# Weight chunks split in pieces, and three stage starts taken row by row, in a two-block attention, convolution and mLSTM kernel

## What is computed

```python
# first block
h   = rms_norm(x, g_pre) * (1 + scale) + shift        # scale, shift, gate = c @ w_ada + b_ada
proj = h @ w_in                                        # queries, keys, values, gates, z, merge
o_a, o_b = attention over compressed, selected and windowed keys, and a second windowed one
y   = (sigmoid(m_a) * ((o_a * silu(z_a)) @ w_o_nsa)
       + sigmoid(m_b) * ((o_b * silu(z_b)) @ w_o_swa)) @ w_out
x   = x + gate * rms_norm(y, g_post)
# second block, on [16 meta tokens; x], 528 tokens
u   = rms_norm(x, norm_w[0])
b, c, xin, z = split(u @ conv_in_w, 4)                 # 1024 -> 4 * 2048
x   = x + (silu(z) * b * causal_conv3(c * xin)) @ conv_out_w
u   = rms_norm(x, norm_w[1]);  x = x + mlstm(u)        # 4 heads, projections 1024 -> 8192
out = rms_norm(x, final_norm_w)[16:]
```

## Time and profile before

| | us |
|---|---|
| median of 3 runs (range) | 1727.71 (1726.42 to 1729.01) |
| the profiled execution, its own time | 1728.46 |
| its span, first to last instruction | 1726.7 |
| PE busy | 1636.3 |
| DVE / POOL / ACT busy | 750.3 / 606.0 / 536.5 |
| mean granted TensorE clock | 0.968 |

### The profile page before, as it was taken

One profiled execution on the slowest core, in us unless ns is written; L12 is line 12 of the kernel. 1 busy time (PEld: TensorE's weight loads), 2 busy tenths in 40 slices (PEclk: granted clock), 3 DMA queues, 4 the chain that ended last, 5 costly groups with the idle time before them and its releaser, 6 DMA issues.

```text
span 1726.7 us, 25059 instructions
## 1 busy us (share of the span) xinstructions
PE 1636.3 (95%) x9782; PEld 1415.2 (82%) x9782; DVE 750.3 (43%) x1489; ACT 536.5 (31%) x842; POOL 606.0 (35%) x485
## 2 busy tenths in 40 slices
PE   5898999999989989999999999989999999999996
PEld 5676777777767789999999999978788778878885
DVE  5705455554565753333233321232632462262255
ACT  2332333233332343222332222232332342233232
POOL 3454212222215423344434344233243244324332
PEclk9999999999989969999999999989999999999998
DMA  8132111111113401222222222222122122112111
GB/s 330 73 115 81 50 49 49 49 49 49 49 73 116 176 25 74 96 97 90 80 83 87 97 82 89 73 74 74 49 80 76 63 73 93 53 51 95 73 49 73
DMA packets 22738, 140.56 MB, mean 81 GB/s; under 512 B 3248, under 2 KB 3248, under 8 KB 6448
## 3 DMA queue, kind: packets, MB, share of 16 engines
q1 hardware_dynamic: 18752, 131.08, 20.6%
q10 hardware_dynamic: 3952, 9.00, 1.4%
HBM read 137.98 MB, written 2.10 MB: 81 GB/s over the span
## 4 chain that ended last, share of the span: by engine, by line
issue 40%; PE 37%; POOL 17%; DVE 4%; ACT 1%; POOLq 0%; DVEq 0%; ACTq 0%
PE lin L365 31%; POOL w_lo L311 17%; PE aux L788 3%; PE aux L760 1%; DVE mix L1466 1%; PE aux L746 1%; ACT w_hi L353 0%; PE aux L442 0%; DVE squares L1484 0%; PE aux L399 0%; PE aux L716 0%; PE aux L748 0%; DVE tmp L1405 0%; DVE residual L1509 0%; ACT mix L1019 0%
## 5 line engine op out<-in xcount | busy, mean ns | idle before, releaser
L311 POOL TENSOR_TENSOR w_lo<-w_raw,w_hi 128x512 fp32r<-128x512 f32 x460 | 602.3, 1341 | 1102.2 <-ACT w_hi L353 1102.2
L365 PE MATMUL lin<-x_hi,w_hi 128*128 128x272 f32 (+1 forms) x2128 | 590.6, 331 | 24.3 <-POOL w_lo L311 17.0
L365 PE MATMUL lin<-x_lo,w_hi 128*128 128x272 f32 (+1 forms) x2128 | 579.4, 326 | 0.0
L365 PE MATMUL lin<-x_hi,w_lo 128*128 128x272 f32 (+1 forms) x2128 | 578.1, 326 | 0.0
L365 PEld LDWEIGHTS lin<-x_hi,w_hi 128*128 128x128 f32 x2128 | 358.7, 192 | 71.1 <-issue 18.2
L365 PEld LDWEIGHTS lin<-x_hi,w_lo 128*128 128x128 f32 x2128 | 358.1, 192 | 32.5
L365 PEld LDWEIGHTS lin<-x_lo,w_hi 128*128 128x128 f32 x2128 | 358.6, 192 | 28.0
L353 ACT ACTIVATE w_hi<-w_raw 128x2048 fp32r<-128x2048 f32 x115 | 219.4, 1909 | 162.1 <-PE lin L365 156.6
L860 ACT ACTIVATE prob<-prob,neg_max 128x31 f32<-128x31 f32 (+6 forms) x128 | 60.1, 471 | 157.5 <-DVE neg_max L1196 157.5
L1317 DVE TENSOR_TENSOR conv_in<-conv_c_gate,lin 128x272 f32<-128x272 f32 (+1 forms) x32 | 12.3, 427 | 213.8 <-PE lin L365 213.8
L365 PE MATMUL lin<-mix,w_hi 128*128 128x512 f32 x256 | 81.9, 401 | 10.6 <-DVE mix L1466 7.1
(11 more groups left out here) (293 smaller groups left out, 1924.4 us busy)
## 6 DMA issues: line engine op xcount, KB each, us to landing
w_raw<-wstream SPq DMA_DIRECT2D x115, 1024.0 KB, 4.8
ada_shift_scale<-w_ada SPq DMA_DIRECT2D x8, 1024.0 KB, 19.1
ada_gate<-w_ada_gate ACTq DMA_DIRECT2D x4, 1024.0 KB, 5.7
residual<-x_t SPq DMA_DIRECT2D x1, 2048.0 KB, 8.9
residual<-x_t ACTq DMA_DIRECT2D x1, 2048.0 KB, 8.4
out_t<-residual ACTq DMA_DIRECT2D x8, 256.0 KB, 2.1
small_inputs<-smalls ACTq DMA_DIRECT2D x1, 537.0 KB, 3.5
residual<-meta_t ACTq DMA_DIRECT2D x1, 64.0 KB, 11.1
```

The lines of the kernel that those rows point to most:

```text
L311: ins = eng.tensor_tensor(wlo[h][:, cols], raw[h][:, cols], whi[h][:, cols].bitcast(F32), ALU.subtract)
L365: ins = t.matmul(o, w[half][:, c0:c0 + P], x(k, t0, cnt), start=(n == 0), stop=(n == 3 * kts - 1))
```

## The change

It makes the weights usable in pieces. ACT's high part becomes 2 instructions of 1024 columns, each with its own count in `s_hi`. POOL's four low parts stay as they are, but each adds 1 to `s_lo`, and POOL waits for the second half of `w_hi` only ahead of its third. PE waits for a piece ahead of each second row k in the first tile of a chunk (each fourth row, or each row, where a chunk has 16 or 4 rows), in place of one wait ahead of the chunk. SP's waits are counted in fours and mean the same.

It takes three stage starts row by row over more tiles. In the first projection both tiles are fed from one row before the next. In wo, the first chunk's tiles m = 0 and m = 1 are, with the second in other PSUM banks. In cin, both tiles of chunk 0 and, three rows behind, the first tile of chunk 1 are, and all this starts when the first row is ready, ahead of the norm. The squares of that norm are then kept (in the space of y), added up on DVE after the last row (eight instructions), turned into a column by PE in the middle of chunk 1's second tile, and spread after it. ACT splits chunk 1 of cin ahead of its work on the rows. DVE's copy of the norm factors of y (L449, there) is gone: it reads them from PSUM and puts the scaled y into PSUM. The first trip of cin is written out, the loop has 7.

The core of the diff, with the same edit elsewhere left out:

```diff
+HIGH_PIECES, PIECES = 2, 4
...
-                    eng.wait_ge(s_lo, i * 2 + (h + 1))
+                    eng.wait_ge(s_lo, i * (2 * PIECES) + PIECES * (h + 1))
...
+            def low_parts(h, first, i=0, per=0):
+                for p in range(PIECES):
+                    if p % (PIECES // HIGH_PIECES) == 0:
+                        eng.wait_ge(s_hi, i * (HIGH_PIECES * per) + (HIGH_PIECES * first + p * HIGH_PIECES // PIECES + 1))
+                    cols = slice(CHUNK // PIECES * p, CHUNK // PIECES * (p + 1))
+                    eng.tensor_tensor(wlo[h][:, cols], raw[h][:, cols], whi[h][:, cols].bitcast(F32),
+                                      ALU.subtract).then_inc(s_lo, 1)
...
-            a.activation(whi[h][:], raw[h][:], ACT.Copy).then_inc(s_hi, 1)
+            for p in range(HIGH_PIECES):
+                cols = slice(CHUNK // HIGH_PIECES * p, CHUNK // HIGH_PIECES * (p + 1))
+                a.activation(whi[h][:, cols], raw[h][:, cols], ACT.Copy).then_inc(s_hi, 1)
...
+            def rows_ready(first, rows, i=0, per=0, then=None):
+                def before(k):
+                    if k % rows == 0:
+                        eng.wait_ge(s_lo, i * (PIECES * per) + (PIECES * first + k // rows + 1))
+                    if then:
+                        then(k)
+                return before
...
+                ready = rows_ready(START["proj"] + c, 2)
+                if first:
+                    for k in range(KD):
+                        ready(k)
+                        eng.wait_ge(s_xlo, k + 1)
+                        for g in range(2):
+                            ins = group(eng, c % 2, g * P, 256, KD, lin_outs(g, TB1), x_hi, x_lo, ks=[k])
...
+            for x in range(2):
+                for k in range(4):
+                    eng.wait_ge(s_og_lo, 4 * x + k + 1)
+                    for m in range(2):
+                        ins = wo_tile(0, m, x, ks=[k])
...
-            growing_totals_pe(eng, n2, TB2, T2)
-            norm_spread_pe(eng, n2, TB2)
+            LAG = 3
+            for k in range(KD + LAG):
+                if k < KD:
+                    eng.wait_ge(s_ulo, k + 1)
+                    for g in range(2):
+                        ins = cin_tile(0, g, ks=[k])
...
+                if k >= LAG:
+                    ins = cin_tile(1, 0, ks=[k - LAG])
+            ins.then_inc(s_cin_tile, 1)
+            cin_tile(1, 1, before=second_norm).then_inc(s_chunk, 1)
+            eng.wait_ge(s_conv_in, 1 + CREDIT)
+            norm_spread_pe(eng, n2, TB2, bank=0)
...
+            chunk_lands_and_splits(eng, START["cin"] + 1)
             for k in range(KD):
                 eng.wait_ge(s_x1, k + 1)
                 act(xhi[:, k, :], res[:, k, :], ACT.Copy, scale=norm_c[:, 0, k:k + 1]).then_inc(s_uhi, 1)
-                if k >= 2:
-                    eng.wait_ge(n2.added, k - 1)
-                act(sq[:, k % 2, :], res[:, k, :], ACT.Square).then_inc(n2.squared, 1)
-            grown_root_act(eng, n2, TB2, D)
+                act(m_a[:, k, :], res[:, k, META:T2], ACT.Square).then_inc(n2.squared, 1)
+            act(meta_sq, res[:, :, 0:META], ACT.Square).then_inc(n2.squared, 1)
...
+            gates_out(0, 0)
+            chunk_lands_and_splits(eng, START["cin"] + 2)
+            norm_root_act(eng, n2, TB2, D, bank=n2_total)
+            conv_out(0, 0)
+            chunk_lands_and_splits(eng, START["cin"] + 3)
+            gates_out(0, 2)
...
-            norm_rstd_dve(eng, own, n1, TB1)
+            eng.wait_ge(n1.spread, 1)
...
-                own.up(stt(tmp[:, k % 2, 0:T1], m_a[:, k, :], gpost[:, k:k + 1], rstd[:, 0:T1], ALU.mult, ALU.mult))
+                own.up(stt(aux[3][:], m_a[:, k, :], gpost[:, k:k + 1], aux[2][:], ALU.mult, ALU.mult))
```

More of the change, by code:

```diff
@@ L497, in project @@
                         eng.wait_ge(s_q, g + 1)
-                    elif not first:
+                    else:
                         eng.wait_ge(s_proj_out, 2 * (at - 1) + g + 1)
-                    ins = group(eng, c % 2, g * P, 256, KD, lin_outs(g, TB1), x_hi, x_lo,
-                                before=(lambda k: eng.wait_ge(s_xlo, k + 1)) if first and g == 0 else None)
+                    ins = group(eng, c % 2, g * P, 256, KD, lin_outs(g, TB1), x_hi, x_lo, before=None if g else ready)
                     ins.then_inc(s_chunk if g else s_proj, 1)
@@ L682, in _, with cin_tile, second_norm, cin_trip @@
             norm_spread_pe(eng, n1, TB1)
-            growing_totals_pe(eng, n2, TB2, T2)
-            norm_spread_pe(eng, n2, TB2)
-            with eng.bass.Fori(0, 8, 1, engines=[eng.engine]) as ii:
-                for c in range(4):
-                    chunk_ready(START["cin"] + c, ii, 4)
+            def cin_tile(c, g, ks=None, before=None):
+                return group(eng, c % 2, g * P, 256, KD, cin_outs(c, g), x_hi, x_lo, ks,
+                             before if g else rows_ready(START["cin"] + c, 2))
+            def second_norm(k):
+                if k == 4:
+                    eng.wait_ge(s_cbc_out, 1)
+                    norm_total_pe(eng, n2, TB2, KD, bank=n2_total)
+            LAG = 3
[4 more added lines that the diff above has]
+                        ins = cin_tile(0, g, ks=[k])
+                        if k == KD - 1:
+                            ins.then_inc(s_chunk if g else s_cin_tile, 1)
+                if k >= LAG:
[4 more added lines that the diff above has]
+            norm_spread_pe(eng, n2, TB2, bank=0)
+            def cin_trip(ii, cs):
+                for c in cs:
+                    ready = rows_ready(START["cin"] + c, 2, ii, 4)
                     for g in range(2):
@@ L695, in _, with last_rows @@
                             eng.wait_ge(s_conv_in, ii * 4 + ({0: -1, 1: 0, 4: 1, 5: 2}[j] + CREDIT))
[L696 to L697 removed]
+                        ins = group(eng, c % 2, g * P, 256, KD, lin_outs(g, TB2), x_hi, x_lo, before=None if g else ready)
                         ins.then_inc(s_chunk if g else s_cin_tile, 1)
+            for g in range(2):
+                eng.wait_ge(s_cbc_out, g + 1)
+                cin_tile(2, g).then_inc(s_chunk if g else s_cin_tile, 1)
+            cin_trip(0, range(3, 4))
+            with eng.bass.Fori(1, 8, 1, engines=[eng.engine]) as ii:
+                cin_trip(ii, range(4))
+            def last_rows(k):
+                if k >= KE - 2:
+                    eng.wait_ge(s_vlo, k + 1)
             with eng.bass.Fori(0, 2, 1, engines=[eng.engine]) as ii:
                 for c in range(4):
[L701 removed]
                     if c < 2:
@@ new lines, in gates_out @@
+            def gates_out(ii, c):
+                u = c // 2
+                for g, dst in ((0, cb), (1, cc)):
+                    if g == 1:
+                        eng.wait_ge(s_chunk, ii * 4 + (START["cin"] + c + 1))
+                    else:
+                        eng.wait_ge(s_cin_tile, ii * 4 + (c + 1))
+                    eng.wait_ge(s_conv, ii * 2 + (u + CREDIT))
+                    for b, t0, n in TB2:
+                        ins = act(dst[:, t0:t0 + n], lin[g][:, b, 0:n], ACT.Copy)
+                    ins.then_inc(s_cbc_out, 1)
@@ L1301, in _ @@
             low_u(KD - 1)
+            eng.wait_ge(n2.squared, 2)
+            own.up(tt(ssum[:, META:T2], m_a[:, 0, :], m_a[:, 1, :], ALU.add))
+            for k in range(2, KD):
+                eng.wait_ge(n2.squared, k + 1)
+                own.settle()
+                own.up(tt(ssum[:, META:T2], ssum[:, META:T2], m_a[:, k, :], ALU.add))
+            own.settle()
+            eng.wait_ge(n2.squared, KD + 1)
+            eng.tensor_reduce(ssum[:, 0:META], meta_sq.rearrange("p k n -> p n k"), AX.X, ALU.add).then_inc(n2.added, KD - 1)
@@ L1340, in _ @@
+                    conv_in(ii, u, [lin[0][:, b, :] for b in range(2)])
+                    conv_rest(ii, u, [lin[1][:, b, :] for b in range(2)])
                 own.leave(8)
```

218 lines of the change are left out of this document (110 added, 108 removed).

## The result

| | before | after |
|---|---|---|
| median of the runs, us | 1727.55 (1726.42 to 1729.01, 4 runs) | 1684.35 (1682.91 to 1686.08, 4 runs) |
| ratio after to before, 95% interval | | 0.975 (0.9739 to 0.9762) |
| profiled execution, us (span) | 1728.46 (1726.7) | 1686.08 (1684.3) |
| mean granted clock | 0.968 | 0.979 |

A forecast was written before the change was run, and what follows sets the result against it. PE's matmul time was taken as the floor, leaving its idle time and half clock to win. Terms 8.0 + 1.6 + 6.3 + 3.9 + 2.2 + 0.8 + 13.1 = 35.9 us gave 1692 us, range 1682 to 1706.

The forecast's parts named there:

- part 4: Start of cin: rows taken up ahead of the norm, PE starting at 610.5 and bound by itself; gain 13.1 us.
- part 3: First chunk of wo: two tiles fed row by row gain 1.85 us, 1.1 lost to DVE; net 0.8 us.
- part 2: First projection: both tiles fed row by row, PE ending at 59.0 instead of 61.2; gain 2.2 us.
- Part 1: Weights in pieces: PE's waits for POOL of 4.18 us at 80.15 and 3.85 at 100.89 both go, 8.0 us.
- 1.6 us at 145.08: First attention group: of a 3.11 us wait for POOL only 1.6 us go, the first exponential being PE's next need.
- 6.3 us for cin's seven waits: Trips 2 to 8 of cin: seven waits for POOL, 0.9 us each by the starts, all go; 6.3 us.
- 3.9 us for the clock behind the long waits: Behind the two long waits in the first block, half-clock losses of 2.2 and 1.7 us go with the idle time.
- Costs at nothing: Some 345 added waits on PE, and ACT's second start of 0.1 us for each of 115 chunks, were costed at nothing.
- A: Rival: the clock stays low through cin's row-by-row start, price 12 us, 1704 us; chance 0.15.
- B: Rival: waits pass to ACT's and DVE's chains, pieces help nowhere, the other parts alone give 16.1 us, 1712; chance 0.08.
- C: Rival: added waits at the first tile of every chunk cost PE, at 0.15 us each 52 us, 1744 us; chance 0.03.
- D: Rival: next to nothing changes, added waits costing 0.1 us each, about 1727 us; chance 0.02.

The follow-up runs named there:

- pair_later: The changed kernel with eight of VectorE's ten small copies of a pair's scalars moved behind its first maxima; 1682.17 us, ratio 0.9736.
- finer_pair: The changed kernel with those eight copies moved behind the first maxima and ScalarE's split in four instructions of 512 columns; 1681.9 us, ratio 0.9732.
- pieces_only: The kernel before with only ScalarE's halves, POOL's quarters signalled one by one and TensorE's row waits; 1700.78 us, ratio 0.9848.
- rows_only_same_code: The changed kernel with whole chunks, TensorE's piece waits kept and met waits added so its mLSTM loop starts at the same program place; 1709.6 us, ratio 0.9902.
- more_waits: The changed kernel with each row's wait of TensorE for pieces written four-fold, all already met; 1699.18 us, ratio 0.9837.
- act_whole: The changed kernel with ScalarE's split in one instruction of 2048 columns, POOL's four pieces and TensorE's waits kept; 1690.93 us, ratio 0.9794.
- rows_only: The changed kernel with chunks whole again: ScalarE splits in one instruction, TensorE waits at the first row for all; 1727.62 us, ratio 1.0.
- moved_code: The changed kernel with some 200 more met waits, all ahead of the mLSTM stage, to move its loop in the program; 1693.76 us, ratio 0.9807.

## Why the prediction was right, and where its terms were not

The mechanism that the prediction names, pieces that let PE start early and stage starts that fill PE, is the one that gained, and the time lies in its range. The medians moved 7.3 us more than the forecast, the profiled spans 6.5 (42.4 against 35.9). Of these 6.5, the table gives 4.7 to places that the prediction put at nothing, 2.0 to cin's trips, 1.2 to part 4, 0.6 to part 3 and 0.3 to the long waits; 0.2 went missing in part 2 and 2.1 at the first exponentials.

- *Part 1, 8.0 us for the two long waits.* 4.4 + 3.9 = 8.3. Right, and started chunks weren't held again.
- *1.6 us at 145.08.* The step that failed. All 3.2 went, but 3.7 were lost by 154.75: net -0.5. The working held the first exponential at 147.05, ending about 148.6, and let PE reach it late at half clock. In truth it hangs on VectorE's maxima, behind ten small copies, and all of this chain starts with PE's own work, so that it can't stay where it was when PE comes early. With PE's group at full clock PE was there early and waited 2.92 us in this trace, 1.44 and 1.26 in two others of the same program, and in all three a stretch at half clock lay behind that wait. With eight of the copies moved behind the maxima (`pair_later`, `finer_pair`) wait and stretch are gone. The prediction's own test, "the waits for POOL coming back as waits for DVE or ACT", had named it as a sign of error.
- *6.3 us for cin's seven waits.* 8.3 over that stage: 5.3 of idle time and 3.0 in which PE is busy less. The cause was read too shallowly: the wait was for POOL, POOL's delay was ScalarE's, and ScalarE's was a table load in each trip, which part 4 removes as well. The term was put in part 1 alone; by `pieces_only` and `rows_only_same_code` either part earns it.
- *3.9 us for the clock behind the long waits.* 2.3 + 1.6 = 3.9.
- *Part 2, 2.2 us.* 2.0 at the compression; in the end 1.3 by the medians and nothing by the spans.
- *Part 3, 0.8 us.* 1.4 by the table, 0.6 within wo by the run without it; the forecast new wait for VectorE of 1.1 us is there with 0.8.
- *Part 4, 13.1 us.* 14.3. PE's start was forecast at 610.5, that is 592.4 less the 18.1 won before; it was 592.25. DVE's first `x_lo` was to take 0.7 us more beside POOL and took 1.38 in place of 0.76. POOL's last low part ended at 591.63, 0.81 us after `x_lo` had begun, and `x_lo` ended 0.57 us after that; in the earlier trace rows the operation of 1.22 us ended 0.55 us after the low part beside it (517.05, then 517.60). The Trainium skill (SBUF — State Buffer, Who interferes with whom) says that the second of two such operations is blocked until the first ends. Both traces agree with that, as far as POOL's rough times can tell. Full clock came 4.25 us after PE's start (5.5 forecast). The fourth chunk waited for POOL, 0.5 us, not 1.2 for ScalarE, and ended 52.1 us after the start, 53.2 forecast. The 1.2 was mis-added: the steps that the prediction lists from 639.1 come to about 12.2 us, 651.3 and not 652.0, so that only 0.5 us of waiting for ScalarE would have been left.
- *Costs at nothing.* TensorE's added waits: 0.002 us each at most, by `more_waits` up to 1203 us. ScalarE's second start: 230 instructions of 1.05 us for 115 of 1.91, in its idle time.
- *Left out.* 0.8 us at the very start, which `act_whole` gives back in part (0.5), so ScalarE's halves have to do with it; and 2.3 us in attention, where the prediction put "nothing". In the traces the third of the half-clock stretches there lasts 6.8 us before (from 412.7) and 3.4 after (from 398.4), which is 1.7 of the 2.3; but it lasts 6.8 in `act_whole` as well, so that this term stays open. From cout on the prediction expected the same lengths, and 1.6 us are gone there, not traced further.

Of the rivals, A (clock low through cin's rows, 1704) falls with the stretch from 596.50 at 1.00; the depth-cycling of PSUM banks, by which the Trainium skill (TensorE: Matmul & The Clock Gate, A second HAM failure mode: psum-queue depth-cycling) would have it hold, did not appear in rows that two or three tiles take up. B (the pieces help nowhere, 1712) would have looked like `rows_only_same_code`, which takes 1709.6; the pieces gave 25 us more. C and D have no cost of a wait to stand on. But a loss was possible in a way that no rival named: had the 786 instructions by which TensorE's program grew put the mLSTM loop in a bad place, 9 to 19 us would have been lost. That it did not come to this was luck.

## What to carry to other kernels

Splitting a staged load into pieces that are signalled one by one, and letting the consumer wait row by row, paid 25 us here at no cost in waits that could be measured; the gain is where PE truly stood and where the clock was low behind that. When a wait names an engine, follow that engine back one step more before giving the gain to one edit: here a table load of ScalarE stood behind POOL's delay. And when a variant that only adds or drops waits comes out slower, look at the packets of the instruction queue and at waits put down to "issue" before believing that the edit itself cost the time.

## What the runs showed of the hardware that was not expected

A long loop on TensorE can load its code anew in each trip, depending on where it stands in the program. The mLSTM loop holds 1526 to 1644 instructions of TensorE in these kernels, as counted in the built programs (a matmul and its weight load are two). Beginning at instruction 4980 of the program it loaded nothing after its first trip (27 packets of 16 KB in all), in the changed kernel and in `rows_only_same_code`. At 4926 (`rows_only`), 5181 (`moved_code`) and 5185 (`more_waits`) it loaded nine packets in each trip behind the first (54, 55 and 55 in all). PE stood 3.5, 1.8 and 2.6 us in the middle of a tile near the trip's start, and the granted clock was 0.75 in the 6.8 us behind it in `rows_only`; that cost up to 7 us a trip (146.7 us became 150.1 and 153.6 at most). The kernel before (4227) and `pieces_only` (4278) had no packets in the trips either, so that their time holds none of this.

The Trainium skill (Runtime: NRT & Kernel Launch, Instruction fetch mechanics) says that a taken branch to code outside the current window of two blocks of 256 instructions forces a fetch before execution goes on. The runs agree in part: where the trips load, PE stands near their head. But the loop is some six such blocks long, and at 4980 the same branch back loads nothing, so that more than two blocks are held there. The same section of the Trainium skill calls the crossing of a block mostly hidden; in the middle of these trips that is so, at their head it is not. What tells good places from bad is open; the three bad ones lie 61 to 65 instructions behind a multiple of 256, the three good ones 116 to 182.
